# Gate and up steps of 512 features with tokens as the stationary operand, in a one-core transformer kernel

## The reference, cut to what matters

```python
def swiglu_ffn(x, w_gu, w_down):          # x 256 x 1024, w_gu 1024 x 5632, w_down 2816 x 1024
    gate, up = jnp.split(x @ w_gu, 2, axis=-1)
    return (jax.nn.silu(gate) * up) @ w_down

x = x + 0.5 * swiglu_ffn(rms_norm(x, ffn1_norm[layer]), ffn1_w_gu[layer], ffn1_w_down[layer])
```

## Time and profile before

| what | us |
|---|---|
| median of 3 runs (lowest, highest) | 2683.52 (2682.12, 2688.59) |
| the profiled execution, its own time | 2680.09 |
| its span in the trace | 2678.3 |
| PE busy | 2560.3 (96%) |
| DVE busy | 1311.5 (49%) |
| ACT busy | 435.4 (16%) |
| POOL busy | 204.2 (8%) |

### The profile page before, as it was taken

How to read it: one execution, slowest core, us unless ns; L and a number is a source line. 1 busy time by engine, 2 the same in 40 slices (tenths; PEclk the granted TensorE clock), 3 DMA queues, 4 the chain that set the end, 5 groups by cost and what they waited for, 6 DMA issues and landing times.

```text
span 2678.3 us, 44222 instructions
## 1 busy us (share of the span) xinstructions
PE 2560.3 (96%) x18150; PEld 1643.6 (61%) x18150; DVE 1311.5 (49%) x2784; ACT 435.4 (16%) x1187; POOL 204.2 (8%) x330
## 2 busy tenths in 40 slices
PE   8999999999999998999999999999999899989996
PEld 8964457797599444477964649945545344634452
DVE  6887442488877955425887556664630000101002
ACT  1201252011012013321101221102310110101010
POOL 3010100000000102000001110001100000000000
PEclk9999999999999999999999999999999999999999
DMA  9684323367656743234675434544359999999997
GB/s 299 205 318 160 110 95 126 117 216 255 214 189 220 252 157 126 82 108 152 217 254 150 136 115 154 186 160 119 113 224 403 412 413 412 417 412 411 409 417 311
DMA packets 306523, 619.18 MB, mean 231 GB/s; under 512 B 15948, under 2 KB 172784, under 8 KB 306192
## 3 DMA queue, kind: packets, MB, share of 16 engines
q1 hardware_dynamic: 287088, 550.80, 55.5%
q0 software_dynamic: 19232, 65.52, 7.3%
HBM read 607.47 MB, written 8.79 MB: 230 GB/s over the span
## 4 chain that ended last, share of the span: by engine, by line
PE 69%; issue 10%; DVE 9%; DMA 6%; SPq 4%; ACT 1%; POOL 1%; DVEq 0%; POOLq 0%; ACTq 0%
PE psum L1293 22%; PE psum L1439 10%; PE psum L1859 6%; PE psum L1482 5%; PE psum L1344 4%; PE psum L1574 3%; DMA xn<-in_w_ada 2%; PE psum L1209 2%; PE psum L1161 2%; PE psum L1770 2%; DMA ring<-in_w_exp_up 2%; PE psum L1880 2%; SPq L822 2%; SPq L823 2%; DVE proj L2915 1%
## 5 line engine op out<-in xcount | busy, mean ns | idle before, releaser
L1439 PE MATMUL psum<-ring,xT 128*32 128x512 f32 (+3 forms) x3372 | 293.0, 494 | 17.3 <-DMA ring<-in_w_exp_up 16.7
L3409 DVE SCALAR_TENSOR_TENSOR proj<-proj,psum 128x256 f32<-128x256 f32 (+1 forms) x63 | 24.9, 395 | 555.1 <-ACT proj L2326 555.1
L1439 PEld LDWEIGHTS psum<-ring,xT 128*32 128x32 f32 x3372 | 128.0, 110 | 168.4 <-issue 111.7
L1293 PE MATMUL psum<-xT,ring 128*128 128x128 f32 x1600 | 195.0, 275 | 0.0
L1293 PEld LDWEIGHTS psum<-xT,ring 128*128 128x128 f32 x1600 | 187.7, 192 | 4.1 <-issue 3.8
L1859 PE MATMUL psum<-ring,xT 128*128 128x384 f32 (+1 forms) x448 | 156.2, 498 | 1.1 <-DVE xT L2550 1.1
L2915 DVE SCALAR_TENSOR_TENSOR proj<-xn,cols,proj 128x512 f32<-128x512 f32 x168 | 126.0, 750 | 18.3 <-DMA xn<-in_w_ada 14.3
L1574 PE MATMUL psum<-ring,memT 128*128 128x512 f32 x256 | 119.3, 605 | 8.2 <-issue 8.1
L943 POOL DMA_DIRECT2D xn<-in_w_ada x96 | 69.5, 726 | 677.0 <-DVE proj L2915 670.4
L1859 PEld LDWEIGHTS psum<-ring,xT 128*128 128x128 f32 x448 | 80.9, 190 | 61.2 <-issue 10.8
L1161 PE MATMUL psum<-ring,y 128*128 128x512 f32 x256 | 113.5, 601 | 0.7 <-ACT kTx L2086 0.7
(11 more groups left out here) (528 smaller groups left out, 4197.9 us busy)
## 6 DMA issues: line engine op xcount, KB each, us to landing
ring<-in_ffn_w_gu SPq DMA_DIRECT2D x88, 1024.0 KB, 7.3
ring<-in_w_exp_down SPq DMA_DIRECT2D x62, 1024.0 KB, 16.9
xn<-in_w_ada POOLq DMA_DIRECT2D x96, 512.0 KB, 4.9
ring<-in_ffn_w_down SPq DMA_DIRECT2D x44, 1024.0 KB, 7.4
ring<-in_w_exp_gate SPq DMA_DIRECT2D x82, 512.0 KB, 11.7
ring<-in_w_exp_up SPq DMA_DIRECT2D x82, 512.0 KB, 15.6
ring<-in_w_exp_gate SPq DMA_DIRECT2D x52, 384.0 KB, 9.8
ring<-in_w_exp_up SPq DMA_DIRECT2D x52, 384.0 KB, 12.4
```

Source lines behind the costliest of these rows:

```text
L1293: ins = mm(banks[bank][:, t * P:(t + 1) * P], weights(t)[:, k, :], tokens[:, k, :], start=(new and t == 0 and k == 0), stop=(k == 3), skip ...
L1439: ins = mm(o[:, :, o0:o1], xg[e % 2][:, k, 32 * g:32 * g + 32], w_[:, :, c0:c1], start=(k == 0 and n_ == 0), stop=(k == KT - 1), skip_grou ...
```

## The change

A feed-forward now has step 0 and five wide steps (`WIDE = 5`) of 512 features. Tokens are stationary (128 of them), and 512 columns move: 256 of gate and 256 of up side by side, which is one unit. A product is 4 matmuls of 128x512 (8 records) instead of 2 x 8 of 128x128 (32 records in two steps). A wide step w has four units, A11, A21, A22, A12 in this order, each loaded by two transfers of 512 KB. Each is released at its own place: A11 by M3, A21 by M7, A22 by M4, A12 by M3. There is one set of S1, S2, S4.

```diff
+WIDE = (NSTEP - 1) // 2
+UNITS = {"A11": 0, "A21": 1, "A22": 2, "A12": 3}
 # release of a slot, in the order of the units
+            released += [("gu_done1", t + 1)] * 2
+            for w in range(1, WIDE + 1):
+                done = t + 1 + 2 * w
+                released += [("gu_done0", done), ("product_done", n["products"] + 7 * w - 1), ("gu_done1", done), ("gu_done0", done)]
...
 # PE, products
-                    for t in range(2):
...
-                        for k in range(4):
-                            ins = mm(banks[bank][:, t * P:(t + 1) * P], weights(t)[:, k, :], tokens[:, k, :],
-                                     start=(new and t == 0 and k == 0), stop=(k == 3), skip_group_check=True)
+                    for k in range(4):
+                        ins = mm(banks[bank][:, :], tokens[:, k, :], weights[:, k * 512:(k + 1) * 512],
+                                 start=(new and k == 0), stop=(k == 3), skip_group_check=True)
...
 # PE, order of the wide steps
+                for w in range(1, WIDE + 1):
+                    products(w, "M1")
+                    if w > 1:
+                        products(w - 1, "M4")
+                        turn_hidden(2 * w - 3)
+                    through_last_bank(2 * w - 1, 0)
+                    products(w, "M5")
+                    through_last_bank(2 * w - 1, 1)
+                    products(w, "M6")
+                    products(w, "M2")
+                    through_last_bank(2 * w, 0)
+                    turn_hidden(2 * w - 2)
+                    products(w, "M3")
+                    through_last_bank(2 * w, 1)
+                    products(w, "M7")
...
 # DVE
+                    if w < WIDE:
+                        weight_sums(w + 1, ("S2",))
+                    dve.wait_ge(sm["part_summed"], summed(n0, w, "U2"))
+                    dve.wait_ge(sm["gu_done0"], t0 + 1 + 2 * w)
+                    V.tensor_tensor(c12_rows, banks[Y][:, :], c12_rows, ALU.add).then_inc(sm["part_summed"], 1)
+                    if w < WIDE:
+                        weight_sums(w + 1, ("S3", "S4"))
+                    else:
                         down_sums(0)
...
+                    first_column(w, 1)
+                    dve.wait_ge(sm["product_done"], produced(n0, w, "M7"))
...
+                    V.tensor_tensor(second_rows, banks[Z][:, :], m1_copy[w % 2], ALU.add).then_inc(sm["part_summed"], 1)
```

```diff
+                    if i < ROW_PAIRS:
+                        link(V.tensor_scalar(rden[:, :, 1], rden[:, :, 1], stat[:, 14:15], None, ALU.mult))
+                        for b in range(NB):
+                            p = p_sb[b][:, :, 0:(b + 1) * P]
+                            link(V.tensor_scalar(p[:, 0, :], p[:, 0, :], rden[:, b, 0:1], None, ALU.mult))
+                            V.scalar_tensor_tensor(p[:, 0, :], p[:, 1, :], rden[:, b, 1:2], p[:, 0, :], ALU.mult, ALU.add)\
...
-                        for h in range(2):
+                        for h in range(1 if i < ROW_PAIRS else 2):
...
-MORE = 3
+MORE = 6
-EXPERT_ORDER = (0, 1, 2, RING, 3, 4, 5, 6, RING + 1, RING + 2)
+EXPERT_ORDER = (0, 1, 2, RING, RING + 3, RING + 2, RING + 4, RING + 5, 3, 4, 5, 6, RING + 1)
+ONCE = EXPERT_RING
```

## The result

The changed kernel takes 2740.9 us (median of 4 runs, 2734.4 to 2751.3) against 2682.9 for the kernel before in the same runs: a ratio of 1.0215, with a 95% interval of 1.0179 to 1.0251. It is 58 us slower. The forecast was 2706 with a range up to 2728: the direction was right, the size was off by 35 us, and the time lies outside the range.

A forecast was written before the change was run, and what follows sets the result against it. PE was taken to bound the kernel up to the experts, DMA transfers within them. Terms summed to +22.7 us on the profiled 2680.1, so 2702.8; the runs' median lies 3.4 higher, giving 2706, range 2660 to 2728 for 8 in 10.

The forecast's parts named there:

- products and turning back: Feed-forwards: wide products save 24 us over 25 wide steps, 220 new PE transposes cost 24 us; together 0.
- waits at M4: First four wide steps: PE waits 2.2 us for U3, queued behind S4 and its late load A12; 20 times, +44 us.
- last wide step: Last wide step: down-projection sums ahead of U3 make PE wait 0.8 us instead of 0.45 at M4; +1.7 us.
- norms: Last transpose to first gate product shrinks from 3.45 to 0.75 us; with the program's start, -9 us, bounds -6 and -11.
- hybrids: Both hybrid stages: fewer transposes and value products, no wait for differential heads; -10 us, bounds -4 and -14.
- experts: Expert layer: four more 1 MB slots filled while SP's queue ran dry; -10 us at the end, bounds -5 and -12.
- constants taken out: 36 products of constants removed where PE would wait: 0 us, bounds -3 and 0; four clock falls, +6, bounds 0 and +20.
- clock behind the waits at M4: Rival, chance 0.08: idle time at M4 lowers the clock; 20 falls of 1.7 us, +34 more, 2740 us.
- the formula quoted beside them: Load of A12: 2.0 us plus bytes at 436 GB/s, 4.4 us for 1 MB; wait 1.5 us, sum +30 instead of +44.
- the 1 us named: Sign for the norms: the first gate product (L1287) starts within 1 us of the last transpose (L1164).

## Why the prediction was right in kind and wrong in size

| term | forecast | shown |
|---|---|---|
| products and turning back | 0 | 429.3 ns a record, 109 a transpose: as forecast |
| waits at M4 | +44 | +50.0 (46.7 idle, 3.3 for the overlap lost), 2.5 of it of another cause |
| last wide step | +1.7 | about +6 |
| norms | -9 | -8.4 (three gaps of 3.45, 3.44 and 3.19 us are 0.94 each; first product of all at 11.3 and not 12.5) |
| hybrids | -10 | -7.4 as changed, -11.5 with constants back |
| experts | -10 | +2.9 and -2.0 as changed (two pairs of traces), -2.4 with constants back; the ring alone -4 |
| constants taken out | 0, and +6 of clock | about +16 |
| clock behind the waits at M4 | 0 (a rival) | about +10 |

With the hybrids and the experts taken from the version that has the constants, the right column adds up to +60; measured +58. The clock and the constants hold 20 of the 35 us that the forecast missed by.

**Right.** The main mechanism, its place and its size. "S4 of the next step needs A12", "PE waits 8.9 - 6.7 = 2.2 us" and "20 times, +44 us" stand: 2.36 us in the row, 46.7 in all, and taking S4 out of U3's way ends it. Some 2.5 us of the 46.7 remain when S4 is moved and are not of this mechanism. The transfer in the chain took 4.96 us, near the 5.1 of the rows; the formula quoted beside them from the Trainium skill (DMA: Bandwidth & Descriptors, section Anatomy of one DMA) is given there for transfers that GpSimd issues, and these are SP's. The products brought nothing by width: 429.3 ns a record, as the row of before had it. The norms' step came out too: from the last transpose to the first gate product 0.94 us remain, under the 1 us named.

**Wrong: the clock, twice.** This is the step that failed. The prediction put the constants at 0 and wrote of the clock "I take four falls that matter, +6". The trace of before has six stretches at half clock, 31 us in all; that of after has 17, 100 us in all, six of them at M4. The one at the start of the second hybrid lasts 10.2 us and costs up to 4, since PE works through 8 of the 10 at half speed, and the one ahead of the experts brings their first product 6.7 us later; a fall was priced at 1.7 "and more after the longer one". The row for this was there: the earlier trace rows shows a stretch of 10.23 us at half clock with 8.82 us of work, behind 0.87 of 3.43. Taking out the constants alone costs 16 us in the kernel before. And the rival "The idle time at M4 takes the clock down (0.08)" was partly true: six of 20 waits, not all, brought the clock down, 10 us instead of its 34. It names 2740, the measured time, and that is luck: it adds 34 us for falls at M4, where about 10 were paid, and nothing for the constants, which cost 16.

**Wrong: the last wide step.** The term was built on M4, "0.8 us instead of the 0.45", with four transposes ahead of it as mere time. But the transposes wait for the gating, which stands behind the same eight sums: 7.4 us of waits (6.0 and 1.4 in the group above), against 1.4 before at M4. I followed the queue to U3 and not to the second reader behind the same sums. Moving the sums takes these waits away and gave 6 to 8 us.

**Wrong: the experts.** "Four more slots of 1 MB are filled in that time" is right, and "10.0 us less at the end" does not follow. A load ahead is worth only what it takes off the end: behind the first expert product the wider ring is worth 4 us, in all traces. In the changed kernel the longer half clock ahead of that product takes them back (24.5 and 21.2 us in the two traces against 17.8 in the first of before).

**Open.** What makes the half clock ahead of the experts long or short. It is 13.7 to 20.5 us in the traces without any constants, 17.1 with those at the experts alone, 10.2 with all but those at the experts, and 3.4 to 10.2 with all of them. So the constants of the stages before count for more there than the four at the experts (2661.7 against 2660.0 us without and with them); which of them do it wasn't tried apart. Also open is why four more MB sent ahead give 4 us and not 10.

## What to carry to other kernels

When an engine works through its queue in order, price each instruction that waits for a load by what stands behind it, and for every reader behind it; one sum moved behind the work that others wait for was worth 59 us here, more than an earlier load (41). Idle time of TensorE costs twice where it is followed by dense work: once as the wait, once by the clock; products of constants in stretches that wait anyway, which look free to remove, gave 16 us. But where the wait is itself avoidable, filling it gave at most some 8 us of the 59 here.

## What the runs showed of the hardware

Between dense products, at waits of 1.9 to 4.6 us, the granted clock fell to its lower level of 1.2 GHz in 6 of 20 places in one execution, for 3.4 us each time, and in 4 of 20 in another, once for 6.8; the length of the wait alone does not tell which, as waits of 2.7 us passed without a fall. Behind stretches with 0.46 and 0.87 us of work in 3.4 it stayed low for 10.2 us. Ahead of the experts it stayed low for 20.5 us although PE was busy for 16.6 of them, in 79 short records; in another execution of the same kernel it was 13.7 us, and the first expert product came 3.3 us sooner. An FP32 product of 128 columns came to two records of 112 ns, one of 256 columns to two of 216, one of 512 to two of 429: the cost here goes with the columns.
